# Second layer's up projection: the fourth weight sum ahead of the gating product, GpSimd's sums started behind block product 7

## What is computed

```python
# D_MODEL = 1024, D_FF = 2816, SEQ = 256, CONV_WIDTH = 3
h = rmsnorm(x, g_mlp[layer]) * (1.0 + scale2) + shift2
up = h @ w_up[layer]                      # (256, 1024) @ (1024, 5632)
u, g = up[..., :D_FF], up[..., D_FF:]
g = causal_depthwise_conv(g, conv_w[layer], conv_b[layer])   # 3 taps along the tokens
x = x + gate2 * ((jax.nn.silu(g) * u) @ w_down[layer])       # (256, 2816) @ (2816, 1024)
```

## Time and profile before

| | |
|---|---|
| time, median of 3 runs | 2010.81 us (2010.53 to 2011.28) |
| the profiled execution's own time | 2010.96 us |
| its span in the trace | 2009.2 us |
| TensorE busy | 1610.1 us (80%) |
| VectorE busy | 708.8 us (35%) |
| ScalarE busy | 298.6 us (15%) |
| GpSimd busy | 114.4 us (6%) |
| chain that ended last | TensorE 53%, DMA 37%, VectorE 7% |

### The profile page before, as it was taken

How to read it: one execution, slowest core, us unless ns; L and a number is a source line. 1 busy time by engine, 2 the same in 40 slices (tenths; PEclk the granted TensorE clock), 3 DMA queues, 4 the chain that set the end, 5 groups by cost and what they waited for, 6 DMA issues and landing times.

```text
span 2009.2 us, 20637 instructions
## 1 busy us (share of the span) xinstructions
PE 1610.1 (80%) x8516; PEld 865.2 (43%) x8516; DVE 708.8 (35%) x1456; ACT 298.6 (15%) x805; POOL 114.4 (6%) x105
## 2 busy tenths in 40 slices
PE   7999999999999899998765565656998765565665
PEld 3466988544679874574221121212574221121211
DVE  1574556977528886264010010101164010010101
ACT  1143000011510000253000010000253000010000
POOL 0000000000023310220000000000220000000000
PEclk9999999999999999999878788887999887787878
DMA  9790888755235542745899999999645999999997
GB/s 342 292 363 12 277 284 297 280 197 178 85 107 177 200 170 88 211 168 235 366 422 421 422 422 422 422 422 411 213 168 231 371 421 422 421 422 422 422 422 311
DMA packets 184333, 599.64 MB, mean 298 GB/s; under 512 B 18752, under 2 KB 77760, under 8 KB 135104
## 3 DMA queue, kind: packets, MB, share of 16 engines
q1 hardware_dynamic: 184014, 598.03, 76.6%
q10 hardware_dynamic: 242, 0.53, 0.1%
HBM read 594.75 MB, written 3.80 MB: 298 GB/s over the span
## 4 chain that ended last, share of the span: by engine, by line
PE 53%; DMA 37%; DVE 7%; ACT 1%; issue 1%; DVEq 0%; POOL 0%; SPq 0%; ACTq 0%; POOLq 0%
DMA extra<-in_w_down 13%; DMA extra<-in_w_up 13%; DMA extra<-in_w_gate 10%; PE ps L1177 9%; PE ps L1528 7%; PE ps L1290 6%; PE ps L1243 6%; PE ps L885 4%; PE ps L1033 4%; PE ps L1428 3%; PE ps L1122 3%; PE ps L1215 2%; PE ps L999 1%; DVE spare L2555 1%; DVE extra L2215 1%
## 5 line engine op out<-in xcount | busy, mean ns | idle before, releaser
L1528 PE MATMUL ps<-ring,wide 128*32 128x512 f32 x2240 | 344.8, 772 | 222.3 <-DMA ring<-in_w_down 90.9
L1528 PEld LDWEIGHTS ps<-ring,wide 128*32 128x32 f32 x2240 | 81.5, 137 | 467.1 <-issue 209.4
L1528 PE MATMUL ps<-extra,wide 128*32 128x512 f32 x784 | 139.4, 846 | 94.4 <-DMA extra<-in_w_down 35.1
L2992 DVE TENSOR_TENSOR wide<-ps,wide 128x512 f32<-128x512 f32 x16 | 10.3, 686 | 512.5 <-PE ps L1528 512.5
L1177 PE MATMUL ps<-hT,ring 128*128 128x256 f32 (+1 forms) x1088 | 183.8, 330 | 0.0
L1177 PEld LDWEIGHTS ps<-hT,ring 128*128 128x128 f32 x1088 | 166.6, 191 | 17.3 <-issue 2.9
L1290 PE MATMUL ps<-ring,hT 128*128 128x512 f32 (+2 forms) x320 | 127.3, 555 | 0.3 <-issue 0.3
L1528 PEld LDWEIGHTS ps<-extra,wide 128*32 128x32 f32 x784 | 31.9, 148 | 200.5 <-issue 85.3
L2997 DVE COPY wide<-ps 128x512 f32<-128x512 f32 x8 | 5.5, 692 | 294.6 <-PE ps L1528 294.6
L2215 DVE SCALAR_TENSOR_TENSOR extra<-ring,sc,extra 128x512 f32<-128x512 f32 x140 | 105.3, 752 | 5.2
L885 PE MATMUL ps<-ring,hT 128*128 128x512 f32 x192 | 87.8, 616 | 2.0 <-ACT hT L1608 2.0
(11 more groups left out here) (362 smaller groups left out, 2032.8 us busy)
## 6 DMA issues: line engine op xcount, KB each, us to landing
ring<-in_w_gate SPq DMA_DIRECT2D x24, 4096.0 KB, 34.0
ring<-in_w_down SPq DMA_DIRECT2D x24, 4096.0 KB, 34.0
ring<-in_w_up SPq DMA_DIRECT2D x22, 4096.0 KB, 33.5
ring<-in_w_mod SPq DMA_DIRECT2D x24, 2048.0 KB, 13.7
ring<-in_w_up SPq DMA_DIRECT2D x44, 1024.0 KB, 7.9
extra<-in_w_gate SPq DMA_DIRECT2D x8, 4096.0 KB, 33.5
extra<-in_w_up SPq DMA_DIRECT2D x8, 4096.0 KB, 34.3
extra<-in_w_down SPq DMA_DIRECT2D x8, 4096.0 KB, 33.6
```

What stands on the lines that cost most here:

```text
L1528: last = mm(ps[bank + n][e * CAP:(e + 1) * CAP, :], lhs[:, k, e * CAP:(e + 1) * CAP], expert_at(n0, e, k % PAIR, n * N), start=k == 0, sto ...
```

## The change

Two orders are changed, for tiles 2 to 10 of the second layer's up projection; no operation is added or removed, and the first layer's order stays.

- **VectorE.** `up_join` now takes a list of the block products to read. For tile j, VectorE reads product 2 and makes the fourth sum directly behind `conv(j - 1)`, and only then does `product(j - 1)` (with its `mod_out`), the accumulates and the rest of the reads. The last tile's product follows its own convolution as before.
- **GpSimd.** From tile 3 on its sums for tile j wait for block product 7 of tile j - 1.

```diff
-                    if j >= 4:
-                        pool.wait_ge(tile_done, b1_used(B1_AT[(1, "up", j - 2)]))
+                    if j >= 3:
+                        pool.wait_ge(*up_block(s, 7, j - 1))
...
-                        if m == 2:
-                            up_fourth(j)
-                            if j in UP_PARTS:
-                                accumulate(*UP_PARTS[j])
-                            if j == UPT - 1:
-                                down_sums(0)
...
+                    else:
+                        up_join(j, UP_READS[:1])
+                        up_fourth(j)
+                        up_gated(j - 1)
+                        if j in UP_PARTS:
+                            accumulate(*UP_PARTS[j])
+                        if j == UPT - 1:
+                            down_sums(0)
+                        up_join(j, UP_READS[1:])
+                        conv(j)
+                        if j == UPT - 1:
+                            up_gated(j)
+                            down_sums(1)
```

More of the change, by code:

```diff
@@ L2587, in up_fourth, with up_join @@
                     tt(w[0][1], w[0][1], s2, ALU.subtract).then_inc(s.up("b1_summed"), 1)
-                def up_join(j):
+                def up_join(j, ms):
                     v = up_joined(j)
                     y = [[v[:, :, f, c * P:(c + 1) * P] for c in range(2)] for f in range(2)]
-                    for m in UP_READS:
+                    for m in ms:
                         src = ps[UP_BANK[m]][:, 0:T].rearrange("p (h t) -> p h t", h=2)
@@ L2636, in _, with up_gated @@
                 late = len(MODS[L]) - EARLY[L]
+                def up_gated(j):
+                    product(j)
+                    if 0 <= j - LAGS[L] < late:
+                        mod_out(EARLY[L] + j - LAGS[L])
                 for j in range(UPT):
[L2638 to L2652, removed]
+                    if j < UP_WHOLE[L]:
+                        if L == 0 and j == UPT - 1:
+                            down_sums(0)
+                        if L and j == 1:
+                            up_rows_sums()
+                            up_second(2)
+                        conv(j)
+                        if L == 0 or j == 0:
+                            up_gated(j)
+                        if L == 0 and j == UPT - 1:
+                            down_sums(1)
+                        if L == 0 and j < late:
+                            accumulate(EARLY[L] + j)
+                    else:
[5 more added lines that the diff above has]
+                        if j == UPT - 1:
+                            down_sums(0)
+                        up_join(j, UP_READS[1:])
+                        conv(j)
+                        if j == UPT - 1:
+                            up_gated(j)
+                            down_sums(1)
                 if L == 0:
```

## The result

The changed kernel takes 1998.8 us (median of 4 runs, 1998.12 to 1999.08) where the kernel before took 2011.05 (median of 4, 2010.53 to 2011.3). The ratio is 0.9939, with a 95% interval of 0.9922 to 0.9956: 12 us faster. The profiled execution took 1999.08 us with a span of 1997.3.

A forecast was written before the change was run, and what follows sets the result against it. TensorE was taken to stall on VectorE's late fourth sum. Tiles 3 to 10 at 100.1 + 2.0 + 1.1, plus 2.1 in tile 2, make 105.3 against 115.22, so 2010.96 - 9.9 = 2001.1 us, range 1999.0 to 2007.5.

The forecast's parts named there:

- the stall of 1.1 us booked in tile 8: Tile 8: the fourth sum meets GpSimd after tile 7's long VectorE round; TensorE stalls 1.1 us, between 0 and 2.
- the 2.1 us booked in tile 2: Tile 2: block product 5 waits for tile 1's product, held up by the fourth sum and GpSimd; 1.1 to 2.1 us, 2.1 taken.
- Tiles 3 to 10 at TensorE's pace (100.1 + 2.0): Eight tiles at TensorE's 12.51 us, 100.1 us, plus 2.0 us for two modulation products, against 115.22 before.
- The clock: Stage: the slow clock after a TensorE gap in tile 7, about 1.7 us lost, does not come back.
- The fourth sum: Tiles 3 to 10: it comes 1.3 us earlier in each tile; TensorE's wait for it is under 2 us in all.
- 0.2 and 0.6 us: Tiles 4 and 6: VectorE's rounds shrink the fourth sum's 3.5 us of slack by about 0.2 and by 0.6.
- The sum: Tiles 3 to 10 103.2 us and 2.1 lost in tile 2, together 105.3 against 115.22: 9.9 us less.
- The lower bound: Whole time 1999.0 us: unknown costs at their low ends, no stall in tile 8 and 1.1 us in tile 2.
- Contention is only moved: Rival 1: GpSimd's contention costs the same elsewhere and VectorE stays the bound; 3.5 us gained, 2007.5 us; chance 0.16.
- the second: Rival 2: the clock falls once more in the new stretch, 1.7 us of the gain lost, 2002.8 us; chance 0.08.
- the third: Rival 3: gain lost behind the stage, where a transfer or tile 10's product is last; 2010.8 us; chance 0.07.
- the slower rival: Rival 4: all four GpSimd instructions of a tile paid in full, 3.7 us; 4.5 us slower, 2015.5 us; chance 0.07.

The follow-up runs named there:

- GpSimd wait alone: Kernel before with only the change's GpSimd wait (sums behind block product 7), VectorE in its old order: 2007.45 us, ratio 0.9978.
- sums of tile 3 early: Changed kernel, but GpSimd's sums for tile 3 run early as before, only tiles 4 to 10 wait for block product 7: 2000.06 us, stage 116.75.
- run with writes only: Kernel before with GpSimd writing zeros in place of its sums (second layer's up projection wrong): 1998.29 us, ratio 0.9946.
- two starting places: Changed kernel with GpSimd's sums started behind block product 2 (2012.41 us) or block product 3 (2002.26 us) of the tile before, not 7.
- start behind block product 2: Changed kernel with GpSimd's sums started behind block product 2 of the tile before, 3.6 us earlier than behind 7: 2012.41 us, ratio 1.0003.
- tripled product: Changed kernel with the product of every tile from 2 on made three times on VectorE, behind the fourth sum: 2015.56 us, ratio 1.0022.

## Why the prediction missed its range

The mechanism of tiles 3 to 10 was right; two terms of the sum were mis-sized, both toward too small a gain: the stall of 1.1 us booked in tile 8, where none came, and the 2.1 us booked in tile 2, where 0.8 were lost.

- **Tiles 3 to 10 at TensorE's pace (100.1 + 2.0).** Right: 102.05 us against 102.1.
- **The clock.** Right: the mean granted clock is 1.00 in the changed stage. TensorE's busy time in tiles 3 to 10 fell by 3.0 us (from 105.05 to 102.04), in which the 1.7 us are contained.
- **The fourth sum.** Right: no wait is left. VectorE stopped standing before the Silu, and the convolution runs at 0.73 + 1.79 us (below).
- **The stall of 1.1 us in tile 8.** Wrong: there is none. The timeline of tiles 7 and 8 in the changed kernel:

```profile
672.93 0.73 DVE L2550 TENSOR_SCALAR spare<-extra,cols 128x256 f32<-128x256 f32 x2
673.70 1.79 DVE L2555 SCALAR_TENSOR_TENSOR spare<-extra,cols,spare 128x255 f32<-128x255 f32 x4
...
676.12 1.22 DVE L2587 TENSOR_TENSOR ring<-ring,extra 128x1024 f32<-128x1024 f32 x1
...
678.65 5.87 DVE L2215 SCALAR_TENSOR_TENSOR extra<-ring,sc,extra 128x512 f32<-128x512 f32 x4
...
679.35 2.95 POOL L2052 TENSOR_TENSOR extra<-ring 128x512 f32<-128x512 f32 x2 [6.47 <-PE ps L1215]
...
682.26 3.39 POOL L2054 TENSOR_TENSOR ring<-ring 128x512 f32<-128x512 f32 x2
...
684.62 0.95 DVE L2607 TENSOR_TENSOR extra<-ps,extra 128x256 f32<-128x256 f32 x2
...
691.69 1.22 DVE L2587 TENSOR_TENSOR ring<-ring,extra 128x1024 f32<-128x1024 f32 x1
...
692.99 2.88 POOL L2052 TENSOR_TENSOR extra<-ring 128x512 f32<-128x512 f32 x2 [7.34 <-PE ps L1215]
...
694.47 1.95 PE L1215 MATMUL ps<-hT,ring 128*128 128x128 f32 x16
```

  The four accumulates took 5.87 us where four at 0.78 take 3.1: 2.75 of contention, three meetings at 0.92. I had charged four; the first of them had ended when GpSimd began, and the last of GpSimd's instructions ran on beside the reads of PSUM at 684.62. The round from one fourth sum to the next was 691.69 - 676.12 = 15.6 us and not 16.6. And the slack had not shrunk ahead of it: in tile 7 the fourth sum still ended 5.5 us after the tile's start (677.34 - 671.89), as worked out for a tile without any delay. I had subtracted 0.2 and 0.6 us for the rounds of tiles 4 and 6. Tile 4's round was 12.72 us, 0.2 over TensorE's 12.51 as worked out, but tile 5's, with two accumulates, was 12.26 and took it back, which the sum left out; tile 6's was 13.31, under TensorE's 13.37, since one of its four accumulates met GpSimd and not two. In tile 8 the sum ended at 692.91, 7.4 us after the start, and was needed at 694.47. The meeting with GpSimd, which began at 692.99, was missed by 0.1, but nothing hung on that: with 0.92 more the sum would still have ended by 693.9.
- **The 2.1 us in tile 2.** Wrong: 14.70 - 13.90 = 0.8. The timeline of tile 2 in the changed kernel:

```profile
613.22 0.41 DVE L2607 TENSOR_TENSOR extra<-ps,extra 128x256 f32<-128x256 f32 x1
...
613.66 1.22 DVE L2587 TENSOR_TENSOR ring<-ring,extra 128x1024 f32<-128x1024 f32 x1
614.42 2.82 POOL L2052 TENSOR_TENSOR extra<-ring 128x512 f32<-128x512 f32 x2 [29.02 <-PE ps L1215]
614.81 0.68 DVE L2562 TENSOR_TENSOR wide<-spare,ps 128x512 f32<-128x512 f32 x1
...
615.54 2.05 PE L1215 MATMUL ps<-extra 128*128 128x128 f32 x16 [1.27 <-DVE wide L2562]
```

  The product of tile 1 ran beside GpSimd's sum in 0.68 us, its usual time; the first of the two L2052 lasted from 614.42 to 616.02. It reads one operand from PSUM (`spare,ps`), which stood in the earlier trace rows, and an instruction of that kind pays nothing, as the read of the earlier trace rows does. I had priced it as one with two operands in SBUF, such as the product of a later tile, which took 1.46 us beside a sum in the run with the GpSimd wait alone. The run with the sums of tile 3 early settles it: 116.75 us with and without the meeting. The rest, 0.8 against 1.1, is that VectorE came to the product 0.2 to 0.3 us sooner than I placed it: the fourth sum ended at 614.88, which is 613.55 if the stage had begun as before the change, where I had 613.7, and the product began 0.07 us ahead of that end.
- **The sum.** 102.05 + 0.80 = 102.85 against 115.22 makes 12.4 us; I had 9.9. The lower bound stands for a gain of 12.0: it had no stall in tile 8, but still 1.1 us in tile 2 where 0.8 were lost. It held nothing for what differs outside the stage from one execution to the next: the stage began at 606.30 and not 604.97, and the stretch behind it was 0.8 us shorter.
- **The rivals.** "Contention is only moved" falls by the run with writes only and the two starting places: what the sums meet decides, by 13 us. No clock below 1.00 and a gain carried to the end answer the second and the third. For the slower rival, the start behind block product 2 is what it described (1 us longer stage than before the change); it was near, 3.6 us away.
- **Idle time and the clock.** In the stage the granted clock fell at TensorE waits of 2.04 us (before, tile 7), 2.52 (GpSimd wait alone), 2.29 and twice 2.56 (start behind block product 2), 3.49 and 4.94 (tripled product). It did not fall at 2.30 us (before, tile 5) and 2.61 (tripled product), nor in any kernel whose longest wait was under 2; the longest of those was 1.93. So the length of one wait does not tell by itself, and what else decides is not shown.

## What to carry to other kernels

Before moving or splitting work between GpSimd and VectorE, list the VectorE instructions in the stretch by where their inputs lie: those that read PSUM ran beside GpSimd's sums for nothing here, while those with two inputs in SBUF, and the convolution's L2550 with one, mostly paid about 0.9 us for each GpSimd instruction of 1.27 us that they met. One that was already running when GpSimd's began often paid nothing: the accumulate at 665.86 in tile 6 of the changed kernel took its 0.75 us though a sum began at 665.98. Give the side work a start that is tied to the producer's progress, so that it falls on the PSUM reads and behind the step on the critical path, and test an earlier and a later start. When adding up the small delays of several rounds, put in the shorter rounds between them too: here tile 5 took back what tile 4 had lost.

## What the runs showed of the hardware

- VectorE's instruction with one SBUF and one PSUM input kept its 0.68 us beside a GpSimd sum, while SBUF to SBUF accumulates went from 0.75 to 1.64, and the product with both inputs in SBUF from 0.69 to 1.46. The Trainium skill, "SBUF — State Buffer", section "Who interferes with whom", says that a VectorE instruction with at most one SBUF input, outside the two-port modes, does not contend with GpSimd; the traces agree, and this is the sentence of that section that I should have applied to the product of tile 1.
- The place of the contention counts for more than its length: starting the same 5.2 us of GpSimd work 3.6 us earlier in each tile lengthened eight tiles by 13.3 us in all, 5.5 of them in TensorE's own busy time with the clock fallen.
